# Ten tile homes, five experts a loop turn, and a gather that streams the features

## The reference, cut to what matters

```
logits = h @ w_router + b_router ; top 4 of 32 experts ; gate = softmax of the four
for every expert e, for its tokens xb:
    gu   = xb @ w_gu[e] + b_gu[e]              # 1024 -> 2048
    gt   = min(gu[:, :1024], 7) ; up = clip(gu[:, 1024:], -7, 7)
    act  = gt * sigmoid(1.702 * gt) * (up + 1)
    y    = act @ w_down[e] + b_down[e]         # 1024 -> 1024
x += sum of gate * y over the experts of a token
```

## Time and profile before

| | us |
|---|---|
| three executions | 1284.48, 1284.67, 1285.79 |
| the profiled execution's own time | 1284.34 |
| its span, first to last instruction | 1282.5 |
| TensorE busy in it | 1252.9 |
| VectorE busy | 443.3 |
| ScalarE busy | 207.2 |
| granted TensorE clock, mean | 0.997 |

### The profile page before, as it was taken

How to read it: one execution, slowest core, us unless ns; L and a number is a source line. 1 busy time by engine, 2 the same in 40 slices (tenths; PEclk the granted TensorE clock), 3 DMA queues, 4 the chain that set the end, 5 groups by cost and what they waited for, 6 DMA issues and landing times.

```text
span 1282.5 us, 20003 instructions
## 1 busy us (share of the span) xinstructions
PE 1252.9 (98%) x8107; PEld 568.2 (44%) x8107; DVE 443.3 (35%) x970; ACT 207.2 (16%) x551; POOL 17.2 (1%) x30
## 2 busy tenths in 40 slices
PE   8999999999999999999999999999999999999997
PEld 6677654576543333334333333333333333333332
DVE  4454334536452232233223323322332333222233
ACT  3542433623420000000000000000000000000000
POOL 0000001100000000000000000000000000000000
PEclk9999999999999999999999999999999999999999
DMA  9611011963369999999999999999999999999996
GB/s 313 253 66 68 1 30 28 323 262 136 132 254 429 425 430 427 429 430 426 431 427 429 429 426 431 427 426 431 427 429 429 427 430 427 429 429 428 429 427 264
DMA packets 48768, 439.06 MB, mean 342 GB/s; under 512 B 8677, under 2 KB 11213, under 8 KB 24058
## 3 DMA queue, kind: packets, MB, share of 16 engines
q1 hardware_dynamic: 48492, 438.32, 82.1%
q10 hardware_dynamic: 238, 0.20, 0.1%
HBM read 435.17 MB, written 3.33 MB: 342 GB/s over the span
## 4 chain that ended last, share of the span: by engine, by line
PE 71%; DMA 25%; DVE 1%; ACT 1%; issue 1%; ACTq 0%; DVEq 0%; SPq 0%
PE bank L1122 68%; DMA weights<-in_w_gu 25%; PE bank L1125 3%; DMA stream<-in_kv_a_norm 0%; ACT stream L643 0%; DVE x L2582 0%; PE bank L1829 0%; ACT scaled L643 0%; ACTq L649 0%; DVE scaled L2444 0%; DVE stats L2341 0%; ACT weights L643 0%; DVE x L2237 0%; DVEq L2623 0%; DVE small_weights L2422 0%
## 5 line engine op out<-in xcount | busy, mean ns | idle before, releaser
L1122 PE MATMUL bank<-weights,small_weights 128*64 128x512 f32 x1360 | 309.7, 597 | 7.3 <-DMA weights<-in_w_gu 6.6
L2582 DVE SCALAR_TENSOR_TENSOR x<-bank,small_weights,x 128x512 f32<-128x512 f32 x160 | 114.1, 747 | 566.0 <-PE bank L1122 566.0
L1122 PEld LDWEIGHTS bank<-weights,small_weights 128*64 128x64 f32 x1360 | 91.2, 136 | 207.2 <-issue 174.3
L1122 PE MATMUL bank<-weights,scaled 128*64 128x512 f32 x704 | 155.9, 595 | 0.0
L643 ACT ACTIVATE scaled<-bank 128x512 f32<-128x512 f32 (+7 forms) x148 | 55.5, 403 | 340.9 <-PE bank L1122 245.2
L1122 PE MATMUL bank<-small_weights,weights 128*128 128x320 f32 (+4 forms) x400 | 110.1, 422 | 0.1
L1122 PE MATMUL bank<-scaled,small_weights 64*128 64x512 f32 (+1 forms) x320 | 108.0, 641 | 0.7 <-ACT scaled L643 0.7
L643 ACT ACTIVATE scaled<-scaled 128x512 f32<-128x512 f32 x32 | 20.2, 630 | 531.9 <-DVE scaled L1958 531.9
L1122 PEld LDWEIGHTS bank<-weights,scaled 128*64 128x64 f32 x704 | 48.8, 137 | 92.0 <-issue 87.7
L1122 PEld LDWEIGHTS bank<-stream 128*128 128x128 bf16 (+2 forms) x2068 | 72.8, 100 | 28.6 <-issue 28.0
L1122 PE MATMUL bank<-stream,small_weights 128*64 128x512 f32 (+2 forms) x360 | 82.6, 583 | 2.2 <-DMA stream<-in_w_gu 2.2
(11 more groups left out here) (216 smaller groups left out, 892.9 us busy)
## 6 DMA issues: line engine op xcount, KB each, us to landing
weights<-in_w_gu SPq DMA_DIRECT2D x85, 2048.0 KB, 30.3
weights<-in_w_down SPq DMA_DIRECT2D x44, 2048.0 KB, 32.0
stream<-in_w_gu SPq DMA_DIRECT2D x21, 2048.0 KB, 31.7
more_weights<-in_w_gu SPq DMA_DIRECT2D x11, 2048.0 KB, 31.3
small_weights<-in_w_gu SPq DMA_DIRECT2D x11, 2048.0 KB, 29.9
small_weights<-in_w_down SPq DMA_DIRECT2D x10, 2048.0 KB, 31.9
more_weights<-in_w_down SPq DMA_DIRECT2D x10, 2048.0 KB, 32.2
weights<-in_w_in SPq DMA_DIRECT2D x3, 2048.0 KB, 13.7
```

The costliest lines, as they stand in the source:

```text
L1122: return pe.matmul(out, lhsT, rhs, start=start, stop=stop)
L2582: dve.scalar_tensor_tensor(xx, PS[bank][:, :], gcur[:, b:b + 1], xx, ALU.mult, ALU.add)\
```

## The change

- **Homes.** Ten homes instead of nine: the sixth home of old in `stream` moves (columns 3840 to 7936), and a tenth follows it (7936 to 12032). The small tables of the router (`KT`) move to `small_weights`, the memory attention's output (`om`) and the router's weights to other places that are free by then. Ten homes and six tiles repeat every five experts, so `TURN` is 5.
- **First loads.** The order follows the new places; the router's weights are loaded behind the conversion of the biases, and the tenth home after the router's last matmul.
- **First refill.** Tile 10 is loaded in two pieces, the first when block 0 of expert 0 is through (`half_used`).
- **First expert.** VectorE multiplies the first two blocks of the gathered rows and signals `xg_first`, then the other six; TensorE waits for the second part at block 2.
- **Gather** (not the first one). S is loaded as the weights and the token rows stream, 512 features each: 12 matmuls on the two 64-column halves and 3 on the full array. The result has slots on partitions, so ScalarE copies it (`xg_rows`), TensorE transposes it in four f32 transposes between the two down tiles, and VectorE multiplies it into `xgT` then.
- **Activations.** The product with the sigmoid comes ahead of the up half's limit.
- **Last tiles.** The last gate/up tile comes in two DMAs and is used block by block; the last down tile comes in three.
- **Stores.** Halves 0, 2 and 4 by SyncE, 1, 3 and 5 by ScalarE.

The diff, cut to its core:

```diff
-        GT, TILES, SLOTN, TURN = 4, 6, 9, 3
-        slot_sb = [W[...] for n in range(6)] + [VK[:, 5888:9984], RH[:, 2816:6912], W2[:, :]]
+        GT, TILES, SLOTN, TURN = 4, 6, 10, 5
+        slot_sb = [W[...] for n in range(6)] + [VK[:, 3840:7936], RH[:, 2816:6912], W2[:, :], VK[:, 7936:12032]]
...
+            first_tiles(TILES, TILES + 1)
+            sp.wait_ge(sem("x2_add"), KD)
+            first_tiles(8, 9)
+            sp.wait_ge(sem("b3_step"), 12)
             load(wr_sb, k_major(w_router[0], 0, KD), "ld_wr")
...
+            sp.wait_ge(sem("lg_mm"), TB)
+            first_tiles(9, 10)
...
+            sp.wait_ge(*at("half_used"))
+            down_piece(1, 0, 0, 2).then_inc(sem("ld_slot0"), 16)
+            sp.wait_ge(sem("tile_used"), 1)
+            down_piece(1, 0, 2, 4).then_inc(sem("ld_slot0"), 16)
+            with sp.Fori(0, SP_TURNS) as i:
+                for n in range(SLOTN + 1, SLOTN + 1 + TURN * TILES):
+                    sp.wait_ge(sem("tile_used"), i * (TURN * TILES) + (n - SLOTN + 1))
+                    dst, name, _ = tile_at(n)
+                    sp.dma_start(dst, tile_rows(...)).then_inc(sem(name), 16)
...
-            for n in range(2 * TB):
+            for n in range(0, 2 * TB, 2):
                 sp.wait_ge(sem("acc_done"), (E - 1) * HALVES + min(n, HALVES - 1) + 2)
-                store_half(n // 2, n % 2)
+                store_half(sp, n // 2, n % 2)
...
# ScalarE
+            def gathered_rows(it):
+                act.wait_ge(sem("act_ready"), it * 2 + 2)
+                act.wait_ge(sem("gather_mm"), it + 2)
+                run(xg_rows, PS[4][:, :]).then_inc(sem("copies_ev"), 1)
...
+            for n in range(1, 2 * TB, 2):
+                act.wait_ge(sem("acc_done"), (E - 1) * HALVES + min(n, HALVES - 1) + 2)
+                store_half(act, n // 2, n % 2)
...
# TensorE
             def gather(n):
                 pe.wait_ge(sem("slots_ready"), n * 2 + 2)
-                gather_pass(ALL_PARTS, True, True).then_inc(sem("gather_mm"), 1)
+                for i in range(3):
+                    for b in range(2):
+                        for side in range(2):
+                            mm(PS[4][half(side), :], S[:, b, 0, :], xparts[:, b, i, 512 * side:512 * side + 512], i == 0 and b == 0, False)
+                for i in range(3):
+                    m = mm(PS[4][:, :], S[:, 2, :, :].rearrange("p a s -> p (a s)"), sparts[:, i, :], False, i == 2)
+                m.then_inc(sem("gather_mm"), 1)
                 slots_to_rows()
+
+            def gathered_to_features(count):
+                pe.wait_ge(sem("copies_ev"), count)
+                for q in range(4):
+                    m = tr(PS[4][:, q * P:(q + 1) * P], xg_rows[:, q * P:(q + 1) * P])
+                m.then_inc(sem("copies_tr"), 1)
...
+                if tiles[GT - 1] is LAST_GU:
+                    pe.wait_ge(sem(LAST_GU[1]), LAST_GU[2])
+                    part(KD - 2, 0)
+                    part(KD - 2, 1)
+                    pe.wait_ge(sem("ld_last_gu"), 16)
+                    part(KD - 1, 0).then_inc(sem("gate_mm"), 1)
+                    part(KD - 1, 1).then_inc(sem("tile_used"), 1)
+                    return
...
                 for n in range(2):
+                    if n and not gathered:
+                        gathered_to_features(it * 3 + 3)
...
# VectorE
-            def rows_in(g):
-                dve.wait_ge(sem("gather_mm"), g + 1)
-                tt(xgT, PS[4][:, :].rearrange("p (k t) -> p k t", k=KD), bcast(c_ffn2, [P, KD, SLOTS], 2), ALU.mult)\
-                    .then_inc(sem("xg_ready"), 1)
+            def rows_in(count):
+                dve.wait_ge(sem("copies_tr"), count)
+                tt(xgT.rearrange("p (a q) t -> p q a t", a=2), PS[4][:, :].rearrange("p (q a t) -> p q a t", q=4, a=2),
+                   bcast(c_ffn2.rearrange("p (a q) -> p q a", a=2), [P, 4, 2, SLOTS], 3), ALU.mult).then_inc(sem("xg_ready"), 1)
...
+                dve.wait_ge(sem("sig_ready"), it + 1)
+                tt(sig_sb, gt_sb, sig_sb, ALU.mult)
                 dve.wait_ge(sem("tile_used"), it * TILES + GT)
-                ts(up_sb, PS[1][:, :], LIMIT, -LIMIT, ALU.min, ALU.max)
-                dve.wait_ge(sem("sig_ready"), it + 1)
-                tt(sig_sb, gt_sb, sig_sb, ALU.mult).then_inc(sem("act_ready"), 1)
+                ts(up_sb, PS[1][:, :], LIMIT, -LIMIT, ALU.min, ALU.max).then_inc(sem("act_ready"), 1)
...
-            rows_in(0)
+            dve.wait_ge(sem("gather_mm"), 1)
+            for k0, k1 in ((0, 2), (2, KD)):
+                m = tt(xgT[:, k0:k1, :], PS[4][:, SLOTS * k0:SLOTS * k1]..., bcast(c_ffn2[:, k0:k1], ...), ALU.mult)
+                m.then_inc(mark("xg_first") if k0 == 0 else sem("xg_ready"), 1)
```

More of the change, by code:

```diff
@@ L273, in trunk_kernel, with loads @@
         b3 = R[0:96, 0:1024].bitcast(BF16)
-        GT, TILES, SLOTN, TURN = 4, 6, 9, 3
-        slot_sb = [W[:, 4 * FF * n:4 * FF * (n + 1)] for n in range(6)] + [VK[:, 5888:9984], RH[:, 2816:6912], W2[:, :]]
+        GT, TILES, SLOTN, TURN = 4, 6, 10, 5
+        slot_sb = [W[:, 4 * FF * n:4 * FF * (n + 1)] for n in range(6)] + [VK[:, 3840:7936], RH[:, 2816:6912], W2[:, :], VK[:, 7936:12032]]
+        def loads(home, end):
+            return (end - home + SLOTN - 1) // SLOTN + (1 if home == 0 and end > SLOTN else 0)
         def tile_at(n):
-            return slot_sb[n % SLOTN], f"ld_slot{n % SLOTN}", 16 * (n // SLOTN + 1)
+            return slot_sb[n % SLOTN], f"ld_slot{n % SLOTN}", 16 * loads(n % SLOTN, n + 1)
+        LAST, LAST_PARTS = tile_at(E * TILES - 1), ((0, 2), (2, 3), (3, 4))
+        LAST_GU = tile_at(TILES * (E - 1) + GT - 1)
+        SP_TURNS = (E * TILES - 4 - SLOTN) // (TURN * TILES)
         def fixed(e):
@@ L292, in extra @@
         def extra(j):
-            return [(slot_sb[t], f"ld_slot{t}", j * 16 + 16 * ((TILES * E - t + SLOTN - 1) // SLOTN + 1)) for t in range(TILES)]
+            return [(slot_sb[t], f"ld_slot{t}", 16 * (j + 1 + loads(t, TILES * E))) for t in range(TILES)]
         xparts = V[:, 0:3072].bitcast(BF16).rearrange("p (b s d) -> p b s d", b=2, s=3)
@@ L376, in trunk_kernel @@
             mem_units.append(([[(qmT[:, j, qs], km_s[:, j, :]) for j in two]], NMEM, False,
-                              [[vm_s[:, i, j * P:(j + 1) * P] for i in range(2)] for j in two], om[:, h:h + 2, qs]))
+                              [[vm_s[:, i, j * P:(j + 1) * P] for i in range(2)] for j in two], om[2][:, h:h + 2, :]))
         CS_AT = 2
@@ L566, in _, with gate_up_piece @@
-            with sp.Fori(0, (E - 2) // TURN) as i:
-                for n in range(SLOTN, SLOTN + TURN * TILES):
-                    refill(n, i)
-            for n in range(SLOTN + (E - 2) // TURN * TURN * TILES, E * TILES):
+            sp.wait_ge(sem("lg_mm"), TB)
+            first_tiles(9, 10)
+            def gate_up_piece(e, t, k):
+                src = w_gu[0, e, 2 * t * P:2 * (t + 1) * P, :].rearrange("(p k) n -> p k n", k=2)
+                return sp.dma_start(tile_at(TILES * e + t)[0][:, 2 * FF * k:2 * FF * (k + 1)], src[:, k, :])
@@ L1857, in gate_up @@
                         pe.wait_ge(sem(tiles[k // 2][1]), tiles[k // 2][2])
+                    if between is not None and k == 2:
+                        pe.wait_ge(sem("xg_ready"), 1)
                     part(k, 0)
                     m = part(k, 1)
+                    if between is not None and k == 0:
+                        m.then_inc(mark("half_used"), 1)
                     if k % 2:
@@ L1874, in gate_up, with down @@
                     between(KD - 2)
-            def down(it, tiles):
+            def down(it, tiles, gathered=0):
                 pe.wait_ge(sem("act_ready"), it * 2 + 2)
@@ L1926, in _ @@
                     expert(i * TURN + (1 + c), turned(i, c))
-            for e in range(1 + (E - 2) // TURN * TURN, E):
+            for e in range(1 + (E - 2) // TURN * TURN, E - 1):
                 expert(e, fixed(e))
+            expert(E - 1, fixed(E - 1)[:GT - 1] + [LAST_GU, tile_at(TILES * E - 2), LAST])
             scatter(E - 1, 0)
```

127 lines of the change are left out of this document (73 added, 54 removed).

## The result

The changed kernel takes 1291.89 us (median of 6 runs, 1290.43 to 1293.94); the kernel before took 1285.47 us on the same chip (6 runs). The ratio is 1.0048, 95% interval 1.0038 to 1.0058. The profiled execution took 1291.61 us (span 1289.7), 7.3 us more than that of before.

What follows compares the result with a forecast made beforehand. The weight stream bounds the late expert stage; the change makes TensorE the bound. Expert stage +4.8, tail +1.4, stores -0.55 sum to +5.6 us on 1284.67: 1290.3 us, range 1280 to 1297 (main case 1286 to 1295).

Steps and rivals of the forecast that it cites:

- the last fourth tile: Last expert's fourth gate/up tile on TensorE: starts at 1263.9 instead of 1259.16, +4.8 us for the expert stage.
- the stores: Result stores at the kernel's end: two queues issue the last ones together, -0.55 us (bounds 0 and -0.6).
- the tail: After the last fourth tile's start: transposes 0.64 us later, then 8.84 instead of 8.07 to the result's copy; +1.4 us.
- TensorE's net: TensorE's work per expert: gather 0.11 us cheaper, four added transposes 0.77; net +0.65 us, period 28.64 us.
- the halved gather: Gather on TensorE: if swapping stationary and streaming sides halved it, net -0.4 us an expert, about 1276.8 us.
- Rivals A: Expert stage: the weight stream stays the bound, net TensorE cost under 0.27 us an expert; 1276.8 us, faster; 16%.
- B: Expert stage: TensorE bounds, but its net cost is near 0.45 us an expert; 1283.9 us, no change; 16%.
- The stream: Weight transfers in the expert stage: late tiles land 7.0 us sooner, the last gate/up tile at 1252.1.
- the half-tile refill: First refill of a home: waits for four pair steps instead of eight, so the stream is 1.72 us sooner.
- the tenth home's 4.89: Weight stream: one tile is loaded early into the added home and leaves the stream, 4.89 us sooner.
- The start of the expert stage: First expert: VectorE hands over two feature blocks instead of all eight, so TensorE starts 0.4 us sooner.
- Rival C: Each expert: the longer way round or the longer turn's branch stops TensorE, 0.3 us each; 1299.6 us; 8%.

Runs made afterwards that it cites:

- ten_mixed: Changed kernel with three of each turn's five gathers put back to the old 60 matmuls and two streamed; 1291.11 us, 1.0042 of the kernel before.
- nine_rest: Changed kernel without the tenth home, the five-expert turn and the new gather with its copy and transposes; 1285.57 us, 0.9997 of the kernel before.

## Why the prediction was right

The bound, the direction and the sum came out as forecast: 1290.3 us against 1291.89, +5.6 us against +7.3 in the profiled executions and +6.4 in the medians. Of the 1.6 us that are missing, 1.0 lie ahead of the last fourth tile and 0.8 in the stores, and the tail took 0.2 less than forecast. By its steps:

- **TensorE's net.** Gather 2.07 forecast, 2.06 measured; so the halved gather that the prediction weighed did not come (its sum was off, too: half of 2.18 saved gives a net of -0.3, not -0.4). The added transposes with their switches 0.77 forecast: the second down tile starts 417.30 - 413.13 = 4.17 after the first, of which eight pair steps of 0.43 are 3.4, so 0.73 to 0.77 is right. Period 28.64 forecast, 28.62 measured. Rivals A (net under 0.27) and B (0.45) are out by that, and the two runs with added transposes show that the price is paid only beyond the slack of 15.0 us.
- **The stream.** That it comes to lie under TensorE's work is right, and its size was not. Forecast were 7.0 us and the last gate/up tile at 1252.1; that tile's second half landed at 1255.47 instead of 1259.11, 3.6 us sooner. Tile 11 was still 5.2 sooner (382.39 against 387.61), and 7.0 in the written-out kernel with the old gather (380.58). In the nine-home kernel the half-tile refill (forecast 1.72) and the early features (0.4) with the other small edits made it 2.1 later; only the tenth home's 4.89 came in full (4.95 between two kernels). The miss had no effect on the time: at 1264.90, when TensorE came to the tile, it had been there for 9.4 us.
- **The start of the expert stage.** Forecast 0.4 sooner; TensorE starts the first expert's tile 0.70 later (365.73 against 365.03). This term failed in the changed kernel's execution. 0.48 of the delay is there already at the first gather's start (361.32 against 360.84). The early handover itself brings what was forecast where the clock is equal: with a granted clock of 0.66 in 360:365, before has 4.19 us from the gather to the first tile and ten_mixed 3.83. In the changed kernel's execution the clock was 0.50 in 362:367, the lower of the two levels (1.2 GHz), where before had 0.85. That took the gain back (4.41 us), and then cost a term that the prediction did not have: the first three blocks took 6.21 us, start to start, and not 5.45, another 0.76. Six other kernels with the same preparation had 0.66 to 0.82 in 362:367, and nine_rest had 0.50, so the preparation alone does not set it. What does stays open.
- **The last fourth tile.** Forecast 1263.9, measured 1264.90, and part of this closeness is luck. The start is off by 1.1 and the slow blocks by 0.76, together 1.9 us late. Against that, the added work was 31 x 0.65 = 20.2 in the forecast and 19.2 in the rows: (1264.90 - 406.42) - 839.8 = 18.7 over 30 periods, and 406.42 - 371.94 against 404.41 - 370.48, 0.55, in the first expert.
- **The tail.** Gate half at +2.84 as forecast; transposes at +6.30, forecast +6.47; copy of the result 8.85 behind them, forecast 8.84.
- **The stores.** Forecast -0.55, measured +0.21 from the copy of the result to the end. The issue itself came as forecast: both queues issue their last store at 1285.35, 5.30 after the copy, where SyncE's last was 5.84 after it (1278.90). But the span ends 4.35 after that issue and not 3.6. The step that failed is that an earlier issue lands earlier: the last store on ScalarE's queue lands 3.90 us after its issue (1289.25), where SyncE's last one before took 3.16 (1282.06). In the written-out kernels it is 3.78 with two queues and 3.19 with one, and their times are the same (1.0014 and 1.0016).
- **Rival C** (the longer turn's branch stops TensorE) does not occur in the changed kernel (its longest period from expert to expert is 28.68 us up to the last expert's) but in three others. The argument against it, that no period in the earlier trace rows is longer at a turn's end, held for a turn of three and said nothing of a longer one. What was overlooked is why the gather had to be rewritten for five experts a turn: with the windows' counts the old gather makes (3355 + 3355) / 520 x 27.99 = 361 TensorE records an expert and the new one (2518 + 2516) / 520 x 28.6 = 277. Five experts are then 1,385 records and not 1,805. (Records that are missing from a trace would make these counts some per cent low.) The tenth home needs a turn of five, the turn needs the short gather, and the short gather costs 0.63 us of TensorE per expert, 19.2 us in all by the rows above, for 15.0 us of slack. The home's gain (0.46% without the transposes, where all the rest of the change with nine homes and the old gather brings nothing) is real and hidden.

None of the kernels that compute all of the reference is faster than the one before. A version that would be must shorten the turn's code to fit and add less than 0.48 us an expert to TensorE; the streamed gather with its four transposes adds 0.63. This was not found here.

## What to carry to other kernels

Work out an engine's slack at the last place where it waits, and divide it by how often the added work is paid before that place: 15.0 us over 31 experts is 0.48 us, and what is added above that counts in full, what is added below it hardly (two transposes, 0.52 us, cost 2.2 us; four, 0.74 us, cost 8.6). When a loop's body grows, look at the instruction queue's packets in a window of late turns: none means that the body stays loaded, a steady count went, in three kernels here, with a gap at each jump and a slower stream. Writing the loop out removed the gap but not the fetches, and these cost this transfer-bound kernel 4.8 us.

## What the runs showed of the hardware

- A turn of 1,084 (before) or 1,385 (after) TensorE records is fetched once and then repeated without a packet; one of 1,637 (two of five gathers new), 1,805 or 2,166 (six old ones) is fetched again in every turn (40, 40 and 42 packets in 650 us) with 2.5 to 3.4 us start to start at each jump back. In packets of 16 KB: written-out code takes 32 in those 650 us, some 23 experts, so 1.4 an expert with the old gather, and the changed kernel's first turn takes one each 25 us (seven from 381.0 to 532.3), 1.13 an expert of 28.6 us. By these, as an estimate, turns of 4.2 and 5.7 packets stay, and turns of 6.5, 7.0 and 8.4 do not.
- The Trainium skill (Runtime: NRT & Kernel Launch, Instruction fetch mechanics) gives TensorE a buffer of 128 KiB, 2,048 instructions, filled in blocks of 16 KiB, and says that a taken branch whose target is not in the current window of two pages stalls. The packets agree with the block (0.66 MB / 40 = 16 KB), and the stall is there. The size does not fit as it stands: a turn of some 5.7 blocks repeats without a packet, which is more than two, and one of some 6.5 blocks does not, which is less than eight.
- The same page of the Trainium skill says of crossing a block that it is "mostly hidden" and of branches that their stall is one reason why kernels "prefer full unrolling where possible". For TensorE's own time the runs agree: written out, there is no gap. For the kernel they do not: 26 fetches more (33 against 7 in 370:1260) went with 4.8 us here (1280.81 to 1285.58), and the stream of weights lost 0.18 to 0.19 us for each packet.
- TensorE: 12 bf16 matmuls of 64 columns stationary and 512 streaming, in pairs on the two column halves, with three on the full array take the time of 60 small ones (2.06 us with the switch, against 2.08 and a switch): both stream 4,608 columns, so here the columns decided and not the count.
- Transposes of 128x128 f32 between matmuls on column halves cost 0.74 us for four with both switches (period 28.73 against 27.99), and 0.52 for two (28.51).
